# Reordering the second half of an output projection, transposed row picking and a shorter expert choice in a Trainium2 encoder block

## The reference, cut to what matters

```
h   = rms_norm(x);  z = h @ w_in
mix = sigmoid(gate_a) * (GLA(z) @ w_branch_gla) + sigmoid(gate_b) * (DSA(z) @ w_branch_dsa)
x   = x + mix @ w_out                                  # the output projection
t   = rms_norm(x)
g_idx    = argmax(t @ w_router_group + b)              # 1 of 4 groups
e_logits = (t @ w_router_expert + b)[group g_idx]      # 8 experts in it
top 2 experts of them; weights = softmax over the 2, times the group's probability
x   = x + sum over the chosen experts of w * (silu(t @ w_gate[e]) * (t @ w_up[e])) @ w_down[e]
```

## Time and profile before

| | us |
|---|---|
| median of 3 runs | 1116.15 (1115.44 to 1116.46) |
| profiled execution: span | 1114.0 |
| output projection, first to last matmul | 587.85 to 640.5 |
| first matmul of product(0) | 655.83 |
| last expert's down product | 1099.89 |
| busy share: PE / DVE / ACT / POOL | 97% / 51% / 30% / 24% |

### The profile page before, as it was taken

The page is one execution under the profiler, slowest core; times in us unless marked ns, Lnnn a source line. Parts: engine busy times, 40 slices in busy tenths (PEclk is TensorE's granted clock), DMA queues, the critical chain, the costliest instruction groups (busy, mean ns, idle before and its releaser), DMA issues.

```text
span 1114.0 us, 12908 instructions
## 1 busy us (share of the span) xinstructions
PE 1086.1 (97%) x5042; PEld 679.3 (61%) x5042; DVE 564.6 (51%) x1042; ACT 333.4 (30%) x598; POOL 266.1 (24%) x176
## 2 busy tenths in 40 slices
PE   6999999999999999999999999999999999999998
PEld 5777788777778887878887843333333333333333
DVE  4432697488870343338996373333333333333334
ACT  6354733333342455551124211111111111111111
POOL 7433344233153344353434010000000000000000
PEclk9999999999999999999999999999999999999999
DMA  7523333224141322236368599999999999999994
GB/s 193 135 77 75 76 76 76 57 60 111 39 114 38 95 57 57 57 97 205 87 214 317 202 377 425 425 421 425 425 426 424 425 423 424 426 424 425 424 422 197
DMA packets 121692, 263.36 MB, mean 236 GB/s; under 512 B 11808, under 2 KB 97824, under 8 KB 104992
## 3 DMA queue, kind: packets, MB, share of 16 engines
q1 hardware_dynamic: 117888, 255.75, 61.4%
q0 software_dynamic: 2352, 4.18, 1.1%
q10 hardware_dynamic: 1392, 2.62, 0.6%
HBM read 262.33 MB, written 4.20 MB: 239 GB/s over the span
## 4 chain that ended last, share of the span: by engine, by line
PE 96%; issue 1%; DVE 1%; DMA 1%; ACT 0%; SPq 0%; DVEq 0%
PE bank L1023 20%; PE bank L627 19%; PE bank L646 14%; PE bank L1037 10%; PE bank L876 8%; PE bank L941 4%; PE bank L1043 3%; PE bank L1044 3%; PE bank L832 2%; PE bank L1010 2%; PE bank L815 2%; PE bank L1029 1%; PE bank L748 1%; PE bank L702 1%; PE bank L762 1%
## 5 line engine op out<-in xcount | busy, mean ns | idle before, releaser
L2017 POOL TENSOR_TENSOR piece_r<-arena,piece_r 128x1024 fp32r<-128x1024 f32 x84 | 202.5, 2419 | 309.8 <-ACT piece_r L1177 309.8
L627 PE MATMUL bank<-piece_r 128*128 128x512 f32 x936 | 232.2, 398 | 0.0
L1023 PE MATMUL bank<-arena,work 128*64 128x512 f32 x1024 | 226.7, 595 | 3.3 <-issue 2.3
L627 PEld LDWEIGHTS bank<-piece_r 128*128 128x128 f32 x936 | 171.1, 188 | 40.3 <-issue 6.9
L1023 PEld LDWEIGHTS bank<-arena,work 128*64 128x64 f32 x1024 | 74.7, 137 | 138.9 <-issue 138.9
L646 PE MATMUL bank<-piece_r 128*128 128x512 f32 x672 | 156.1, 392 | 0.0
L646 PEld LDWEIGHTS bank<-piece_r 128*128 128x128 f32 x672 | 125.3, 188 | 32.0 <-issue 6.4
L1860 DVE TENSOR_TENSOR arena<-bank,arena 128x512 f32<-128x512 f32 x126 | 80.8, 684 | 104.1 <-PE bank L1044 103.7
L1177 ACT ACTIVATE piece_r<-arena 128x1024 fp32r<-128x1024 f32 x84 | 88.4, 1057 | 100.9 <-DMA arena<-w_branch_gla_in 52.0
L1885 DVE SCALAR_TENSOR_TENSOR bias<-bank,slot_sc,bias 128x256 f32<-128x256 f32 x32 | 15.5, 484 | 159.7 <-ACT bias L1409 159.7
L2092 POOL DMA_INDIRECT arena<-x_rows,idx_pair x15 | 15.0, 998 | 335.9 <-PE bank L1010 301.1
(11 more groups left out here) (265 smaller groups left out, 1158.9 us busy)
## 6 DMA issues: line engine op xcount, KB each, us to landing
arena<-w_exp_gate_in SPq DMA_DIRECT2D x29, 2048.0 KB, 28.1
arena<-w_exp_up_in SPq DMA_DIRECT2D x29, 2048.0 KB, 24.9
arena<-w_exp_down_in SPq DMA_DIRECT2D x21, 2048.0 KB, 27.7
arena<-w_in_in SPq DMA_DIRECT2D x68, 512.0 KB, 4.3
wdn_spare<-w_exp_down_in SPq DMA_DIRECT2D x11, 2048.0 KB, 29.1
arena<-w_branch_gla_in SPq DMA_DIRECT2D x8, 512.0 KB, 4.1
arena<-w_branch_dsa_in SPq DMA_DIRECT2D x8, 512.0 KB, 5.4
arena<-w_out_in SPq DMA_DIRECT2D x2, 2048.0 KB, 12.0
```

The source lines that it names most:

```text
L627: last = mm(bank[n % 2][:, :], w[:, k, :], h[:, k, :], start=(i == 0 and k == 0), stop=(i == 2 and k == K - 1))
L1023: last = mm(onto[hf * WIDE:(hf + 1) * WIDE, :], hTe[q][:, k, :], both[:, :, k, hf * HALF:(hf + 1) * HALF], start=(k == 0), stop=(k == K - 1))
L2017: Q.tensor_tensor(quarter(w_lo, q), quarter(w_raw, q), quarter(w_hi, q).bitcast(F32), ALU.subtract).then_inc(s["wlo_ready"], 1)
```

## The change

Three edits, cut to their core.

1. Order of half 1 of the output projection on PE, and of the steps on DVE:

```
-            for t in range(T):
-                out_pass(T + t, LOW_W, range(K // 2))
-                if t >= 1: x2_transposes(t - 1, 1)
-                out_pass(T + t, LOW_W, range(K // 2, K))
-                if t >= 1: router_logits(t - 1, 0); router_logits(t - 1, 1)
-                out_pass(T + t, HIGH, range(K))
-                if t >= 2: ranks(t - 2)
-            x2_transposes(T - 1, 1)
-            router_logits(T - 1, 0)
-            first_rows(0); ranks(T - 2); router_logits(T - 1, 1)
-            for t in range(T - 1): tokens_of_slots(t)
-            first_rows(1); ranks(T - 1); first_rows(2); first_rows(T - 1); tokens_of_slots(T - 1)
+            out_pass(T, LOW_W, range(K));       out_pass(T + 1, LOW_W, range(K))
+            out_pass(T, HIGH, range(K));        out_pass(T + 2, LOW_W, range(K))
+            x2_transposes(0, 1)
+            out_pass(T + 3, LOW_W, range(K))
+            router(0)                           # router_logits(0, 0) and (0, 1)
+            out_pass(T + 1, HIGH, range(K));    out_pass(T + 2, HIGH, range(K // 2))
+            x2_transposes(1, 1); ranks(0)
+            out_pass(T + 2, HIGH, range(K // 2, K))
+            router(1)
+            out_pass(T + 3, HIGH, range(K // 2))
+            x2_transposes(2, 1)
+            out_pass(T + 3, HIGH, range(K // 2, K))
+            router(2); ranks(1); x2_transposes(3, 1)
+            router_logits(3, 0); ranks(2); router_logits(3, 1)
+            first_rows(0); first_rows(1); ranks(T - 1)
+            for t in range(T - 2): tokens_of_slots(t)
+            first_rows(2); first_rows(T - 1)
+            for t in range(T - 2, T): tokens_of_slots(t)
# DVE
+            add(T); add(T + 1); choose_group(0); choose_experts(0); add(T + 2); place(0)
+            choose_group(1); add(T + 3); choose_experts(1); choose_group(2); choose_experts(2)
+            place(1); choose_group(3); place(2); choose_experts(3)
# SP: load(5) goes behind the last LOW_W pass (low_pass_used 3), no more behind the last HIGH pass
+            sp.wait_ge(s["low_pass_used"], 3)
+            load(5)
             sp.wait_ge(s["x_out_ready"], 2 * T)
-            load(5)
             load_down(2)
             load(6)
```

```
-                for hf in range(2):
-                    last = mm(bank[5 + hf][:, :], first_sel[:, t].rearrange("p q r -> p (q r)"),
-                              x2[:, t, hf * BLK:(hf + 1) * BLK], start=(t == 0), stop=(t == T - 1))
+                for k in range(K):
+                    last = mm(bank[4 + k // 4 * 3][:, k % 4 * P:(k % 4 + 1) * P],
+                              x2[:, t, :].rearrange("p (q k) -> p k q", k=K)[:, k, :],
+                              first_sel[:, t].rearrange("p q r -> p (q r)"),
+                              start=(t == 0 and k % 4 == 0), stop=(t == T - 1), skip_group_check=True)
```

```
-                st.did(V.tensor_copy(gid[:, t:t + 1], i8[:, t, 0:1]))
-                st.did(V.tensor_scalar(tg[:, t, :], lg[:, t, 0:G], v8[:, t, 0:1], None, ALU.subtract))
-                st.did(V.tensor_scalar(pen[:, 0, :], gio[:, :], gid[:, t:t + 1], NEG, ALU.not_equal, ALU.mult))
-                st.did(V.tensor_tensor(le[:, t, :], le[:, t, :], pen[:, 0, :], ALU.add))
+                st.did(V.tensor_tensor(pen[:, 0, :], gio[:, :], i8[:, t, 0:1].to_broadcast([P, NE]), ALU.not_equal))
+                st.did(V.scalar_tensor_tensor(le[:, t, :], pen[:, 0, :], NEG, le[:, t, :], ALU.mult, ALU.add))
...
-                st.did(V.tensor_copy(eid[:, :, t], i8[:, t, 0:TOP_E]))
-                for k in range(TOP_E):
-                    st.did(V.tensor_scalar(oh[:, k, t, :], eio[:, :], eid[:, k, t:t + 1], None, ALU.is_equal))
+                st.did(V.tensor_tensor(oh[:, :, t, :], eio[:, :].unsqueeze(1).to_broadcast([P, TOP_E, NE]),
+                                       i8[:, t, 0:TOP_E].unsqueeze(2).to_broadcast([P, TOP_E, NE]), ALU.is_equal))
```

More of the change, by code:

```diff
@@ L942, in out_pass @@
                               start=(first and k == 0), stop=(last_one and k == K - 1))
-                if last_one:
+                if last_one and K - 1 in ks:
                     last.then_inc(s["x_out_ready"], 1)
-                if i == LOW_MIX and t == T - 1:
-                    last.then_inc(s["low_mix_used"], 1)
+                if t == T - 1 and (i == LOW_MIX or i == LOW_W and hf == 1):
+                    last.then_inc(s["low_pass_used"], 1)
             for k in range(K):
@@ L980, in first_rows @@
                     pe.wait_ge(s["last_sel_ready"], 1)
-                for hf in range(2):
-                    last = mm(bank[5 + hf][:, :], first_sel[:, t].rearrange("p q r -> p (q r)"),
-                              x2[:, t, hf * BLK:(hf + 1) * BLK], start=(t == 0), stop=(t == T - 1))
-                if t == T - 1:
-                    last.then_inc(s["rows_ps"], 1)
+                for k in range(K):
[3 more added lines that the diff above has]
+                              start=(t == 0 and k % 4 == 0), stop=(t == T - 1), skip_group_check=True)
+                if t == T - 1:
+                    last.then_inc(s["xg_T"], 1)
+            out_pass(T, LOW_W, range(K))
+            out_pass(T + 1, LOW_W, range(K))
+            out_pass(T, HIGH, range(K))
+            out_pass(T + 2, LOW_W, range(K))
+            x2_transposes(0, 1)
+            out_pass(T + 3, LOW_W, range(K))
+            router(0)
+            out_pass(T + 1, HIGH, range(K))
+            out_pass(T + 2, HIGH, range(K // 2))
+            x2_transposes(1, 1)
+            ranks(0)
+            out_pass(T + 2, HIGH, range(K // 2, K))
[3 more added lines that the diff above has]
+            out_pass(T + 3, HIGH, range(K // 2, K))
+            router(2)
+            ranks(1)
+            x2_transposes(3, 1)
+            router_logits(3, 0)
+            ranks(2)
+            router_logits(3, 1)
             def slot_scales():
@@ L997, in _ @@
             first_rows(0)
[L998 to L1001, removed]
             first_rows(1)
             ranks(T - 1)
+            for t in range(T - 2):
+                tokens_of_slots(t)
             first_rows(2)
             first_rows(T - 1)
-            tokens_of_slots(T - 1)
+            for t in range(T - 2, T):
+                tokens_of_slots(t)
             def gather_transposes(b, done, ks=range(K)):
@@ L1727, in choose_experts @@
                     .then_inc(s["maskb_ready"], 1)
[L1728 to L1732, removed]
             def place(t):
@@ L1766, in _ @@
                 add(n)
[L1767 to L1777, removed]
+            add(T)
+            add(T + 1)
+            choose_group(0)
+            choose_experts(0)
+            add(T + 2)
+            place(0)
+            choose_group(1)
+            add(T + 3)
+            choose_experts(1)
+            choose_group(2)
+            choose_experts(2)
+            place(1)
+            choose_group(3)
+            place(2)
+            choose_experts(3)
+            st.did(V.tensor_tensor(tg[:, :, :], lg[:, :, 0:G], v8[:, :, 0:1].to_broadcast([P, T, G]), ALU.subtract))
+            st.did(V.tensor_tensor(wt[:, 1, :], top_e[:, :, 1], top_e[:, :, 0], ALU.subtract))
             st.settle()
@@ L1796, in _ @@
                 .then_inc(s["rsg_ready"], 1)
[L1797 to L1800, removed]
             for q in range(2):
@@ L1803, in _ @@
                 evict_gathered(q, s["he_ready"])
+                if q == 0:
+                    dve.wait_ge(s["idx_ps"], 1)
+                    V.tensor_scalar(idx_pair[:, :], bank[1][:, 0:PAIRS_E], float(S), None, ALU.add)\
+                        .then_inc(s["idx_ready"], 1)
             st.did(V.tensor_scalar(tok_pair[:, 0, :], bank[1][:, 0:PAIRS_E], float(S), None, ALU.add))
@@ L2078, in spread, with tokens_of @@
                                        oh[:, choice, t, 0:2].unsqueeze(2).to_broadcast([P, 2, WIDE]), ALU.mult)
+            def tokens_of(t):
+                pool.wait_ge(s["maskb_ready"], t + 1)
+                for k in range(TOP_E):
+                    last = Q.tensor_scalar(tok_of[:, t, k].rearrange("p q e -> p e q"),
+                                           oh[:, k, t, :].rearrange("p (e q) -> p e q", q=2), tok_less[:, t:t + 1],
+                                           None, ALU.mult)
+                last.then_inc(s["tok_of_ready"], 1)
             for t in range(T - 1):
+                tokens_of(t)
                 pool.wait_ge(s["placed"], t + 1)
```

33 lines of the change are left out of this document (12 added, 21 removed).

## The result

The changed kernel takes 1129.08 us (median of 4 runs, 1128.08 to 1129.80) against 1115.80 us before (4 runs, 1115.42 to 1116.46): a ratio of 1.0114, interval 1.0102 to 1.0127. It is 13.3 us slower. The profiled span went from 1114.0 to 1127.5 us.

The account below looks back on a forecast made before the run. The end follows the DMA stream, whose restart product(0) frees. Product(0) 0.9 us later, less 0.5 us for fewer outstanding bytes, gives +0.4 on 1116.15: 1116.5 us, range 1112.8 to 1119.5.

Parts of the forecast that it names:

- What bounds the kernel: Late experts run at the DMA stream's pace; the end is the stream's end plus a fixed tail, its restart freed by product(0).
- outstanding bytes: Bytes still queued at the restart behind product(0): about 0.87 MB against 1.07 MB before, taken as -0.5 us.
- The price of first_rows as it becomes: Row picking with strided weight loads on PE: 16 loads at 0.112 us, 1.79 us a tile, no dearer than before.
- rival A: Slower: strided float32 weight loads in first_rows cost more; 1118.7 us at 0.145 a load, 1121.8 at 0.19; chance 0.21.
- the rule: Trainium skill on SBUF cachelines: full rate needs two hits in a 16-byte line; first_rows' step of 32 bytes has one.
- the steps removed: Wait, copy and transposes behind first_rows, ahead of product(0), gone: 2.24 us.
- The new waits: PE waits for DVE's choice at ranks(0), ranks(1) and ranks(2): 2.2, 0.9 and 1.8 us.
- the walk: Each engine's list laid end to end with prices from the trace, from 618.8 us to product(0) at 656.7.
- The sum: Product(0) 0.9 us later, less 0.5 us for the stream: end +0.4 us, 1116.5 us.
- Rival B: Faster: new waits don't arise or are filled, removed work comes off whole; product(0) 2.9 us sooner, 1112.8 us; chance 0.14.
- Rival C: Faster: stream bound by bytes alone from 641 us, so early load(5) is worth 4.9 us, 1111.2 us; chance 0.05.
- Leaner choice and `tok_of` on POOL: DVE's expert choice 1.50 us, 0.78 us a tile saved on its chain; `tok_of` fits POOL's idle time.

Follow-up runs that it names:

- step4: Changed kernel with first_rows' weights taken every fourth column (within blocks of 512) instead of every eighth: 1128.79 us, ratio 1.0114 to the kernel before.
- rows_only: Kernel before with the transposed row picking (edit 2) alone, old orders, old expert choice, load(5) late: 1122.32 us, ratio 1.0058.
- ranks_later_rows: Changed kernel with ranks(0) and ranks(2) moved later and the row picking of before: 1117.50 us, ratio 1.0010 to the kernel before.
- ranks_later: Changed kernel with ranks(0) moved behind router(1) and ranks(2) behind router_logits(3, 1), strided loads kept: 1122.73 us, ratio 1.0059 to the kernel before.
- waits_filled: Changed kernel with PE's two waits filled by unused matmuls, nine ahead of ranks(0), two ahead of ranks(2): 1125.71 us, ratio 1.0081 to the kernel before.
- step1: Changed kernel with first_rows' weights taken as contiguous blocks of 128 columns instead of every eighth column: 1122.65 us, ratio 1.0052 to the kernel before.
- pair0_layout: Kernel before with leaner choice, early load(5), transposed picking from contiguous blocks, gate and up matrices of experts 0 and 1 reordered to fit: 1114.67 us, ratio 0.9986.
- load5_only: Kernel before with only SP's wait for load(5) moved behind the last LOW_W pass of half 1: 1116.44 us, ratio 0.9998.
- choice_only: Kernel before with the leaner expert choice (edit 3) alone, `tok_of` on POOL: 1115.46 us, ratio 0.9994.

## Why the prediction was wrong, point by point

- **What bounds the kernel: right.** The end follows product(0). Over the kernels whose product(0) comes at 660 or later the two move together within 2 us (step4 is the furthest: 10.8 us at product(0), 12.6 in time). The small excess (13.5 us at product(30) for 12.4 us at product(0)) I had with the other sign, -0.5 us: I took outstanding bytes off, but the stream started from an empty queue. In the 12 us from its restart on it moved less than the 386 GB/s of before:

```profile
670.00:682.00 12.00, 12.00 (x86) 5.35 (x84) 6.58 (x29) 1.76 (x2) 1.16 (x2) 1.00 0.94 359
```

  That is 0.3 MB or 0.8 us less, an estimate. It isn't load(5) early alone that empties the queue: in rows_only, with load(5) late, product(31) starts 6.4 us later (1092.43 for 1086.01) for 5.1 us at product(0).
- **The price of first_rows as it becomes: wrong, the step that failed first.** I put 0.112 us on a load and 1.79 us on a tile, from the row of eight strided transposes; measured are 0.24 us and 3.9 us. 64 loads by 0.13 us are 8.3 us: rival A's mechanism. Rival A's upper end (0.19, unoverlapped) was too low as well. That row isn't of this form, and it was set beside the wrong neighbour: strided loads of transposes beside plain loads of a product. Beside plain loads of transposes it does show a price, 194 ns a record for 140 (line, engine and operation, count, busy us, mean ns):

```profile
L1010 PEld LDWEIGHTS bank<-ident,arena 128*128 128x128 f32 x128 | 15.6, 194 | 11.9 <-issue 11.4 <-DVE arena L1798 0.5
L886 PEld LDWEIGHTS bank<-ident,arena 128*128 128x128 f32 x32 | 3.7, 140 | 2.1 <-DVE arena L1688 1.6
```

  In a row the difference is small (eight in 0.97 us, four plain ones in 0.42), while the float32 product's loads doubled; why the forms differ stays open. I had the rule at hand and let a row of another form outweigh it. ranks_later_rows against ranks_later measures the term net of the steps removed: 4.9 us at product(0), so about 7 us gross, at partly lower clock.
- **The new waits: right in place and size.** ranks(0) was forecast to wait 2.2 us and waited 2.0; ranks(2) 1.8 and waited 1.6; ranks(1) found PE already late. HIGH 1 and load(5) came within 0.4 us of the walk (load(5) at 628.88 for 628.6).
- **What follows a wait: missed.** I priced a wait at its length. Its follow-up, the passes and router products at 1.2 GHz, costs more: load_down(2) went at 643.70 instead of the forecast 640.8, and the last router product ended near 650.9 instead of 647.55, 3.4 us. waits_filled shows that the first pause is the cause of the first fall: with it filled, load_down(2) went at 641.12, so 2.6 of the 3.4 us are shown. The other 0.8 fit the second stretch of lower clock, whose cause is open: the last eight router instructions took 1.74 us there (0.91 in waits_filled, at full clock). No term of the sum and no rival had the clock in it, though the rows showed only pauses up to 0.8 us in that stretch before and so gave no ground to assume 1.00 behind one of 2 us.
- **The sum.** Forecast +0.9 at product(0), measured +12.4: 8.3 from the loads, 3.4 from the clock ahead of first_rows, less about 0.2 elsewhere. These are terms against the forecast and not what each edit gives back: step1 gives back 6.2, because plain loads too are slower at half clock.
- **Rival B** (no new waits, the removed steps whole) didn't come, since the waits arose. pair0_layout has no new waits and plain loads: it reaches 2.6 of B's 2.9 us at product(0), but only 1.5 of its 3.4 us in time. **Rival C** (bytes alone) has no support: in load5_only load(5) went 3.6 us sooner for a ratio of 0.9998 (0.9989 to 1.0007).
- **Leaner choice and `tok_of` on POOL: right**, a little better than priced: choice_only brings 1.06 us at product(0), and DVE's choice of tile 0 took 634.20 to 635.64, 1.44 us, for 1.50 forecast. That POOL doesn't slow DVE is not shown by it. In the changed kernel `tok_of` (0.73 us for its two products) ran while DVE was idle or in instructions with one operand or with an input in PSUM. Where POOL's products of 128 columns for `first_sel` ran beside the choice of tile 3, an instruction of DVE with both inputs in SBUF took twice as long as for tile 0:

```profile
634.43 0.19 DVE L1724 SCALAR_TENSOR_TENSOR work<-work 128x32 f32<-128x32 f32 x1
...
652.83 0.76 POOL L2085 TENSOR_TENSOR work<-bias,work 128x128 f32<-128x128 f32 x2 [1.76 <-DVE bias L1754]
652.88 0.40 DVE L1724 SCALAR_TENSOR_TENSOR work<-work 128x32 f32<-128x32 f32 x1
```

  That choice took 1.77 us instead of 1.44. It cost nothing here, since PE was in first_rows until 658.6 us.

## What to carry to other kernels

A step in the operand that a weight load reads belongs in the price of a matmul: with one float32 element per 16 bytes a load cost double (7.54 us for 32), while two per 16 bytes cost little (3.85 for 3.65). If the order of the features can be changed in an operand that is read once, as the gate and up matrices of experts 0 and 1 are in pair0_layout, do it there. Price an operation by a row of its own form, and if there is none, let the range take the rule that speaks against you. A pause of PE of 2 us can cost more than 2 us: put work in it, or move the waiting instruction behind work that is ready, and read the granted clock behind it.

## What the runs showed of the hardware that was not expected

- A float32 weight load of 128 x 128 takes 0.11 to 0.12 us in a row at steps of 1 and 2 elements and 0.24 us at steps of 4 and 8. At granted clock 0.50 the loads with step 8 keep their pace (32 in 7.73 us at mostly 0.50, in 7.70 us at 1.00), while those with step 1 don't (5.54 and 3.65 us): with one element per 16 bytes it isn't TensorE's clock that bounds them.
- The granted clock also fell with hardly a pause ahead of it: in rows_only it was 0.50 from 649.2 to 652.6 us, after 8 us of strided loads and short products with PE busy all along; there the strided loads hid it (16 in 3.89 us, as in 3.88 at 1.00).
- Issuing a load of 2 MiB 3.6 us sooner was worth nothing, when the queue ran empty behind it (load5_only: 16 GB/s at 655 to 656 us, ratio 0.9998).
- An instruction of DVE with both inputs in SBUF took 0.40 us instead of 0.19 beside POOL's products of 128 x 128.
